# Two-direction SSD in a two-block network: one decay matrix from C.B masked twice, in place of a logarithm and mask matmuls

## The reference

```python
a_cs = jnp.cumsum(a_dt, axis=-1)
xdt = x * dt[..., None]
decay = segsum_exp(a_dt)          # exp(a_cs[l] - a_cs[s]) where s <= l, else 0
cb = jnp.einsum('bclgn,bcsgn->bcgls', c, b)
y_diag = jnp.einsum('bcgls,bcgrls,bcsgrp->bclgrp', cb, decay, xdt)
```

## Time and profile before

| | |
|---|---|
| median of 3 runs | 1795.68 us |
| the profiled execution | 1796.72 us |
| its span, first to last instruction | 1794.5 us |
| TensorE busy | 1771.6 us, 99% |
| VectorE busy | 834.1 us, 46% |
| ScalarE busy | 832.1 us, 46% |
| POOL busy | 811.4 us, 45% |
| mean granted clock of TensorE | 0.998 |

### The profile page before, as it was taken

The page is one execution under the profiler, slowest core; times in us unless marked ns, Lnnn a source line. Parts: engine busy times, 40 slices in busy tenths (PEclk is TensorE's granted clock), DMA queues, the critical chain, the costliest instruction groups (busy, mean ns, idle before and its releaser), DMA issues.

```text
span 1794.5 us, 26559 instructions
## 1 busy us (share of the span) xinstructions
PE 1771.6 (99%) x8872; PEld 1486.0 (83%) x8872; DVE 834.1 (46%) x1476; ACT 832.1 (46%) x1775; POOL 811.4 (45%) x598
## 2 busy tenths in 40 slices
PE   8999999999999999999999999999999999999998
PEld 7888888887888888888888888878888888888887
DVE  4687887878304554235440044050063312355763
ACT  4655555555425665325332233254534442367662
POOL 4553444466443222434654455445364444543322
PEclk9999999999999999999999999999999999999999
DMA  5732221221233221423333333324232223322211
GB/s 181 136 100 63 67 70 60 68 61 58 71 105 112 77 71 54 146 82 94 97 102 95 97 102 95 94 82 167 80 106 89 86 83 94 106 64 70 71 48 59
DMA packets 46227, 159.90 MB, mean 89 GB/s; under 512 B 4764, under 2 KB 7196, under 8 KB 45885
## 3 DMA queue, kind: packets, MB, share of 16 engines
q1 hardware_dynamic: 38592, 140.53, 25.3%
q10 hardware_dynamic: 7548, 18.20, 4.0%
HBM read 152.42 MB, written 6.29 MB: 88 GB/s over the span
## 4 chain that ended last, share of the span: by engine, by line
PE 86%; DVE 6%; issue 4%; ACT 2%; DMA 1%; POOL 0%; DVEq 0%; ACTq 0%; POOLq 0%
PE main L307 63%; PE main L335 6%; PE aux L810 3%; PE main L1875 2%; PE aux L797 2%; DVE u_acc L2081 1%; PE aux L657 1%; PE aux L379 1%; PE aux L781 1%; PE aux L780 1%; PE aux L665 1%; PE aux L1964 1%; PE aux L630 1%; PE aux L633 1%; DVE x_res L571 1%
## 5 line engine op out<-in xcount | busy, mean ns | idle before, releaser
L270 POOL TENSOR_TENSOR w_lo<-raw,w_hi 128x512 fp32r<-128x512 f32 x504 | 688.0, 1373 | 865.3 <-ACT w_hi L266 860.7
L266 ACT ACTIVATE w_hi<-raw 128x512 fp32r<-128x512 f32 x486 | 303.5, 630 | 653.1 <-PE main L307 646.7
L307 PE MATMUL main<-w_hi,a_hi 128*128 128x512 f32 x736 | 304.5, 414 | 1.4 <-ACT gu L1627 0.9
L307 PE MATMUL main<-w_hi,a_lo 128*128 128x512 f32 x736 | 287.8, 391 | 0.0
L307 PE MATMUL main<-w_lo,a_hi 128*128 128x512 f32 x736 | 287.1, 390 | 0.0
L307 PE MATMUL main<-a_hi,w_hi 128*128 128x512 f32 x576 | 230.7, 401 | 0.3 <-DVE relu L2280 0.3
L307 PE MATMUL main<-a_hi,w_lo 128*128 128x512 f32 x576 | 224.8, 390 | 0.0
L307 PE MATMUL main<-a_lo,w_hi 128*128 128x512 f32 x576 | 224.3, 389 | 0.0
L307 PEld LDWEIGHTS main<-w_hi,a_lo 128*128 128x128 f32 x736 | 138.1, 188 | 30.1
L307 PEld LDWEIGHTS main<-w_hi,a_hi 128*128 128x128 f32 x736 | 138.6, 188 | 27.2 <-issue 2.0
L307 PEld LDWEIGHTS main<-w_lo,a_hi 128*128 128x128 f32 x736 | 138.9, 189 | 22.9
(11 more groups left out here) (344 smaller groups left out, 3069.6 us busy)
## 6 DMA issues: line engine op xcount, KB each, us to landing
raw<-w_stream_in SPq DMA_DIRECT2D x264, 512.0 KB, 3.6
x_res<-x_in ACTq DMA_DIRECT2D x8, 512.0 KB, 5.3
rel_rows<-rel_row ACTq DMA_DIRECT2D x1, 4096.0 KB, 44.4
bias<-rel_rows ACTq DMA_DIRECT2D x2, 1536.0 KB, 7.8
out<-x_res SPq DMA_DIRECT2D x4, 512.0 KB, 2.6
bgate<-b_gate_in ACTq DMA_DIRECT2D x4, 256.0 KB, 5.4
ln_g<-ln_g_in ACTq DMA_DIRECT2D x1, 1024.0 KB, 6.2
ln_b<-ln_b_in ACTq DMA_DIRECT2D x1, 1024.0 KB, 9.6
```

The lines of the kernel that those rows point to most:

```text
L266: eng.activation(w_hi[:, k, :], raw[:, k, :], ACT.Copy).then_inc(hi_done, 1)
L270: eng.tensor_tensor(w_lo[:, k, :], raw[:, k, :], w_hi[:, k, :].bitcast(F32), ALU.subtract).then_inc(lo_done, 1)
L307: mm = eng.matmul(mb[m][:, :], lhs, rhs, start=(first and k == 0 and n == 0), stop=(last and k == KT - 1 and n == 2))
```

## The change

The decay matrix is built from the smaller of the two unmasked arguments. Forward and backward arguments have opposite signs off the diagonal, and on it both are 0; so the smaller one is the valid one of its side, and on the diagonal it is 0 and counts for both. The logarithm of dt, its clamp, the identity copy and the two mask tiles go, and so do the two L630 matmuls of each head. `cs_sb` is now the negated cumulative sum.

C.B is multiplied by the upper and by the lower mask, both with the diagonal, as it is read from bank 3: `mask_cb` has two operations of 128x512 where `take_cb` had a copy and seven small ones. ScalarE's new `scale_cb` multiplies the first by the forward dt, in four activations of 128x128 for each head, into a first half of `dmat[r]`, which is now two tiles. VectorE's `weigh` adds the second times the backward dt, in four operations of 128x128, waits for its own end, and then multiplies by the decay. POOL takes `d_skip` from the parameters and no longer waits for `skip_set`.

In ScalarE's order `scale_cb` of the next group's head 0 stands before the turned X tiles, of head 1 before argument 2, of head 2 after exponential 1; head 3's comes after argument 3 of the group itself. Buffers move within the space of the stage. The core of the diff:

```diff
-            for dr, neg in enumerate((neg_f, neg_b)):
-                eng.matmul(ab[dr][:, :].rearrange("p (c l) -> p c l", c=NT), ident_r[:, :],
-                           neg[:, :].unsqueeze(1).broadcast_to((P, NT, P)), start=True, stop=False)
+            for dr in range(2):
                 one_row = picked[:, half, dr, r:r + 1].broadcast_to((P, P))
-                x = eng.matmul(ab[dr][:, :], one_row, cs_hl[:, :], start=False, stop=True)
+                x = eng.matmul(ab[dr][:, :], one_row, cs_hl[:, :], start=True, stop=True)
...
-                pool.wait_ge(skip_set, g + 1)
+                skip = par[:, bass.ds(g * R + PC["d_skip"], R)].unsqueeze(1).unsqueeze(3).broadcast_to((P, NT, R, HP))
...
-            act.wait_ge(clamped, 1)
-            act.activation(ln_dt[:, :, :], sp_t[0][:, :, :], ACT.Ln).then_inc(ln_set, 1)
...
+            def scale_cb(g, r):
+
+                act.wait_ge(cb_set, g + 1)
+                if not (isinstance(g, int) and g == 0):
+                    act.wait_ge(y_full, g * 4 + (r - 3))
+                for c in range(NT):
+                    cs = slice(c * P, c * P + P)
+                    x = act.activation(dmat[r][:, 0, cs], cb_m[:, 0, cs], ACT.Copy, scale=dt_sb[:, c, bass.ds(g * R + r, 1)])
+                x.then_inc(cb_scaled, 1)
...
             decay_exp(0, 0)
             decay_exp(0, 1)
+            scale_cb(0, 0)
+            scale_cb(0, 1)
+            scale_cb(0, 2)
...
                 decay_exp(g, 2)
                 take_arg(g, 3)
+                scale_cb(g, 3)
...
                     slots(11, 12)
+                    scale_cb(g + 1, 0)
                     take_turned(g + 1, 2)
                     take_turned(g + 1, 3)
+                    scale_cb(g + 1, 1)
                     take_arg(g + 1, 2)
                     decay_exp(g + 1, 1)
+                    scale_cb(g + 1, 2)
...
-            dve.tensor_scalar(t[0], dt_sb[:, :, :], 1e-37, None, ALU.max).then_inc(clamped, 1)
-            dve.tensor_scalar(ident_r[:, :], ident, 1.0, None, ALU.mult).then_inc(neg_set, 1)
-            dve.tensor_scalar(neg_f[:, :], mask_u, -NEG, NEG, ALU.mult, ALU.add).then_inc(neg_set, 1)
-            dve.tensor_scalar(neg_b[:, :], mask_u, NEG, None, ALU.mult).then_inc(neg_set, 1)
...
-            def take_cb(g):
+            def mask_cb(g):
 
                 dve.wait_ge(turned, g * 4 + 2)
-                dve.tensor_copy(cb[:, :], ab[3][:, :]).then_inc(aux_free[1], 1)
...
+                for dr, mask in enumerate((mask_u, mask_l)):
+                    i = dve.tensor_tensor(cb_m[:, dr, :].rearrange("p (c l) -> p c l", c=NT), ab[3][:, :].rearrange("p (c l) -> p c l", c=NT),
+                                          mask.unsqueeze(1).broadcast_to((P, NT, P)), ALU.mult)
+                    i.then_inc(aux_free[1] if dr else cb_set, 1)
...
                 def weigh(r):
+                    dve.wait_ge(cb_scaled, g * 4 + r + 1)
+                    for c in range(NT):
+                        cs = slice(c * P, c * P + P)
+                        x = dve.scalar_tensor_tensor(dmat[r][:, 0, cs], cb_m[:, 1, cs], dt_sb[:, c, bass.ds(g * R + (NH + r), 1)],
+                                                     dmat[r][:, 0, cs], ALU.mult, ALU.add)
+                    ch(x)
                     dve.wait_ge(decay_done, g * 4 + r + 1)
-                    dve.tensor_tensor(dmat[r][:, :], cb[:, :], dmat[r][:, :], ALU.mult).then_inc(t_done, 1)
+                    dve.tensor_tensor(dmat[r][:, 0, :], dmat[r][:, 0, :], dmat[r][:, 1, :], ALU.mult).then_inc(t_done, 1)
```

More of the change, by code:

```diff
@@ L154, in two_blocks @@
         c_st = at("c_st", B0 + 6 * KB, [P, TOK])
[L155 to L159, removed]
+        cb_m = at("cb_m", B0 + 8 * KB, [P, 2, TOK])
         sz = at("sz", B0 + 12 * KB, [P, NT, NCOL])
-        dmat = [at(f"dmat{h}", B0 + (22 + 4 * h) * KB, [P, TOK]) for h in range(R)]
+        dmat = [at(f"dmat{h}", B0 + (20 + 4 * h) * KB, [P, 2, TOK]) for h in range(R)]
         xw = at("xw", B0 + 44 * KB, [P, 2, NT, GW])
@@ L665, in pe_y @@
                 x = eng.matmul(ab[c // 2][:, (c % 2) * GW + r * HP:(c % 2) * GW + r * HP + HP],
-                               dmat[r][:, c * P:c * P + P], x_tok[:, c, r * HP:r * HP + HP], start=True, stop=True)
+                               dmat[r][:, 0, c * P:c * P + P], x_tok[:, c, r * HP:r * HP + HP], start=True, stop=True)
             x.then_inc(y_full, 1)
@@ L2085, in conv, with arg_min @@
                             ch.count(ins)
-            def take_cb(g):
+            def mask_cb(g):
                 dve.wait_ge(turned, g * 4 + 2)
-                dve.tensor_copy(cb[:, :], ab[3][:, :]).then_inc(aux_free[1], 1)
-                dve.wait_ge(aux_free[1], g * 5 + 1)
-                dve.tensor_copy(dt_b[:, :, :], dt_sb[:, :, bass.ds(g * R + NH, R)])
-                for c in range(NT):
-                    own = dve.tensor_tensor_reduce(cb_own[:, c, :], cb[:, c * P:c * P + P], ident, 1.0, 0.0, ALU.mult, ALU.add, cb_d[:, c:c + 1])
-                ch(own)
-                ch(dve.tensor_tensor(skip[:, :, :], cb_d[:, :].unsqueeze(2).broadcast_to((P, NT, R)), dt_b[:, :, :], ALU.mult))
-                dve.tensor_tensor(skip[:, :, :], skip[:, :, :], par[:, bass.ds(g * R + PC["d_skip"], R)].unsqueeze(1).broadcast_to((P, NT, R)),
-                                  ALU.add).then_inc(skip_set, 1)
-            def arg_max(g, r):
+                for dr, mask in enumerate((mask_u, mask_l)):
+                    i = dve.tensor_tensor(cb_m[:, dr, :].rearrange("p (c l) -> p c l", c=NT), ab[3][:, :].rearrange("p (c l) -> p c l", c=NT),
+                                          mask.unsqueeze(1).broadcast_to((P, NT, P)), ALU.mult)
+                    i.then_inc(aux_free[1] if dr else cb_set, 1)
+            def arg_min(g, r):
                 dve.wait_ge(arg_in, g * 4 + (r + 1))
                 for c in range(NT):
-                    e = dmat[r][:, c * P:c * P + P]
+                    e = dmat[r][:, 1, c * P:c * P + P]
                     x = dve.scalar_tensor_tensor(e, ab[1][:, c * P:c * P + P], cs_sb[:, c, bass.ds(g * R + (NH + r), 1)], e,
-                                                 ALU.add, ALU.max)
+                                                 ALU.add, ALU.min)
                 x.then_inc(arg_done, 1)
             conv(0, 0, 0)
-            arg_max(0, 0)
+            arg_min(0, 0)
             conv(0, 0, 1)
-            arg_max(0, 1)
-            take_cb(0)
+            arg_min(0, 1)
+            mask_cb(0)
             def group_ms(g0, g1):
@@ L2161, in take_off @@
                         ch(dve.tensor_tensor(y, y, off_t[:, n % 2, :], ALU.add))
-                arg_max(g, 2)
+                arg_min(g, 2)
                 weigh(0)
-                arg_max(g, 3)
+                arg_min(g, 3)
                 weigh(1)
@@ L2196, in ssd_group @@
                 if not last:
-                    arg_max(g + 1, 0)
+                    arg_min(g + 1, 0)
                 dve.wait_ge(bank_free, gp * 12 + (4 * O_Z + 4))
@@ L2201, in ssd_group @@
                 if not last:
-                    arg_max(g + 1, 1)
-                    take_cb(g + 1)
-            per = len(TILES) * 3 + 2 + 2 + 3 + 6 + 1
+                    arg_min(g + 1, 1)
+                    mask_cb(g + 1)
+            per = len(TILES) * 3 + 4 + 2 + 3 + 6 + 1
             with dve.Fori(0, 3) as gp:
```

16 lines of the change are left out of this document (5 added, 11 removed).

## The result

The changed kernel takes 1848.28 us (median of 4 runs, 1847.12 to 1850.10) against 1795.74 of the kernel before (4 runs): ratio 1.0295 [1.028, 1.031], 52.5 us slower. The forecast was 1836, range 1809 to 1858. The profiled execution took 1850.1 us with a span of 1848.3, at a mean granted clock of 0.982.

The account below looks back on a forecast made before the run. Bound: TensorE, 99% busy, beside an equally long loop through ScalarE and VectorE. Groups add 36.9 us, less 0.9 at the start, plus 4 of blocking: +40 on 1796.72 gives 1836.7, 1.0 over the median, so 1836; range 1809 to 1858.

Parts of the forecast that it names:

- a second loop of equal length: In the SSD stage: `pe_arg(1)`, 13.3 us of ScalarE, 29.8 us of VectorE, `pe_turn(1)`; work added there is paid in full.
- zero slack at its end: At `pe_turn(1)`, start 213.97: TensorE waits for VectorE's last off-diagonal read, ended 213.84, with nothing to spare.
- TensorE alone: Rival: only TensorE's work decides, so 64 mask matmuls less save 14.7 us, giving 1781; chance 0.05.
- ScalarE's term: Scaling of three heads queued before `take_arg(3)`, 1.15 us a head, makes it 3.45 us later.
- VectorE's term without blocking: Four added operations and a wait per weighing, 1.27 us a head; heads 1, 2 and 3 in the loop: 3.81 us.
- the blocking by POOL: VectorE's added operations with two SBUF inputs lose time beside POOL: 4 us in all, between none and 12.9.
- already paid: In even groups POOL's catch-up was said to be in the 3.31 us of two weighings, so blocking was taken nearer to none.
- The place of the stall: TensorE idle before L646, `pe_off(0)` and `pe_arg(3)`, released by VectorE, some 8 us in an even group.
- the clock rival: A 3.3 us stall at `pe_off(0)` in even groups halves TensorE's clock: +12 over four groups, 1848; chance 0.10.
- an L646 with no more idle time than now: Sign of being wrong: no added TensorE idle time before the C.B matmul.
- A clock below 1.0: Sign of being wrong: a granted clock below 1.0 in the SSD stage.
- The mask gain: Mask matmuls between `pe_turn(1)` and `pe_arg(1)` save 0.46 us a group, and 0.9 more in the first group: 4.6 us.

Follow-up runs that it names:

- adds_early: The changed kernel with VectorE's additions of heads 0 and 1 moved ahead of the third argument, same work: 1840.78 us, ratio 1.0252.
- gap_scale2: The changed kernel with head 0's addition before the third argument, head 1's before the fourth, and ScalarE's scaling of head 2 behind the fourth: 1840.97 us, ratio 1.0251.

## Why the prediction was right, and where it was off

**The sign and the mechanism held.** The reasons were a second loop of equal length through ScalarE and VectorE, and zero slack at its end. The masks alone gave nothing, the two halves of the added work added up (13.1 + 37.3 against 51.4), all of it lies in the SSD stage, and the odd groups' idle time before the convolution is gone (9.2 us in four waits in the kernel before, group 0's among them; no such wait after). An even and an odd group together are 12.3 us longer (groups 2 and 3: 7.4 + 4.9), forecast 10 to 11. TensorE alone (1781) was not right for the changed kernel even with most of the blocking away (1803.6); it came near only for the masks alone, and only then (1777.8).

**ScalarE's term was right, by two errors that cancel.** 3.45 us forecast, 3.49 measured in group 2, where ScalarE works without a pause. But the 1.15 per head was read as the length of a row of four; what a queue pays is start to start, 1.00 for `take_arg` (190.79 to 191.79). The scaling is 1.17 (187.50 to 188.67), dearer by 0.17 for four, 0.04 each. The Trainium skill, VectorE: DVE Perf Modes, section on the TRN2 errata, has 52 cycles more for a ScalarE read from SBUF than from PSUM, by an estimate from its figures 0.04 us; the trace agrees (0.04, or 397 against 362 ns).

**VectorE's term without blocking** was a little high: from an addition's start to the product's it is 1.16 or 1.17 us (203.76 to 204.92), not 1.27; for three heads and 8 groups some 2.4 us less.

**The step that was mis-sized is the blocking by POOL.** I took 4 us, between 0 and 12.9, "nearer to none". The two stretches of the loop, measured as above in every group, show where it went: ScalarE's from the start of `take_arg(1)` to the end of `take_arg(3)`, and VectorE's from the start of its last argument to the end of the last states. The numbers say by how much a stretch is longer than before, in us; the last column is the growth of the blocking within VectorE's.

| group | ScalarE, forecast | ScalarE, measured | VectorE, forecast | VectorE, measured | blocking, more by |
|---|---|---|---|---|---|
| 0 | 2.6 | 2.1 | 3.2 | 3.0 | 0.0 |
| 1, 3, 5 (each) | 2.5 | 2.2 | 1.0 | 4.5 | 3.9 |
| 2, 4 (each) | 3.5 | 3.5 | 3.8 | 4.6 | 1.1 |
| 6 | 3.5 | 3.5 | 3.8 | 7.9 | 5.5 |
| 7 | 2.2 | 2.0 | 3.8 | 6.1 | 3.0 |
| sum | 22.8 | 21.1 | 21.3 | 39.7 | 22.4 |

VectorE's stretches are 18.4 over the forecast, ScalarE's 1.6 under it, and the half clock ahead of the output panel adds 1.1: 17.9, as many as are missing. That it closes to a tenth is partly luck, for these stretches are not the whole loop. But the pattern of the first table is there: the odd groups and the last two are the ones that were priced too low.

The additions are a part of it: over 0.34 us each they lose 19.3, 11.5, 4.2 and 0 us for heads 0, 1, 2 and 3. Head 0's falls where VectorE waits anyway; heads 1 to 3 have 15.7 in the loop. The rest is in operations that were there before: in group 6 the first convolution runs 10.07 us instead of 5.36, since POOL's work now lies beside it, and in the odd groups the convolution loses 2.1 instead of 1.1 and a product of the states 1.1 instead of none.

The reason for taking 4 was that POOL's catch-up in even groups was "already paid" in the two weighings. There it held: in groups 2 and 4 the weighings of VectorE's stretch lost 2.3 us before, and they and the additions together lose 2.1 now. What failed is that I carried it over to the other groups. In groups 1, 3 and 5 the weighings lost next to nothing before, and the additions lose 2.2; in group 7 the weighings lost 2.8, and they and the additions lose 6.9. The Trainium skill, SBUF — State Buffer, section Who interferes with whom, was the better guide: by its rule I had 1845, and 1848 was measured; L2099 against L2122 and the run with POOL only writing agree with it. The 12.9 us behind that 1845 were a price from other operations, so that it came so near is partly luck too.

What is shown is that with little blocking the same added work costs 25.8 instead of 51.4 us.

**The place of the stall was wrong.** I put it at the C.B matmul (`pe_turn(1)`), some 8 us in an even group together with `pe_off(0)` and `pe_arg(3)`; only the clock rival had a figure for `pe_off(0)`, 3.3. It is at `pe_off(0)`: 4.16 us in group 2, with 1.06 at the fourth argument, 0.68 at the third turn and 0.60 at the third states, 6.5 together. `pe_turn(1)` starts at 232.33, 0.98 after VectorE's read was done at 231.35, and between the two TensorE works through its own stretch without a wait. I had named an L646 with no more idle time than now as a sign that I was wrong. It was a bad sign to choose: two stations of the same loop lie 13.5 us apart, and either can carry the wait.

**The clock fell, and cost nearly nothing.** The rival was right in its event (4.2 to 6.3 us of standstill in seven groups, then 1.2 GHz; with group 7 54.6 us of the stage in all) and its 12 us were wrong: with 37.5 of the 54.6 us back at full clock the time is the same. The other 17.1 us were not tested; 1.1 us in group 7 can be seen to be paid. A clock below 1.0 was the other sign that I had named as one against me, and it proved nothing either.

**The mask gain** (4.6 us) can't be found alone. Taken out alone, the masks leave VectorE's and POOL's work in other places against each other, and the blocking grows by 14 us.

What stays open: how it comes about which of VectorE's and POOL's operations fall together. Edits of the queues that do the same work moved the blocking between 63 us (`adds_early`) and 82 (`gap_scale2`), against 72 in the changed kernel, which is as much as most of the edits were worth. No version found here beats the kernel before with the whole computation in it.

## What to carry to other kernels

An engine that is busy 99% can hide a second loop of the same length through other engines: before work is moved off it, measure the time from one of its hand-overs round to the next, and look for a place where the wait is zero. Price an added operation by what it takes in the company that it will have (here 0.62 us where 0.34 is its free time), and count starts, not lengths, in a queue. Ask of each added operation whether its inputs are both in SBUF and what the other engine that reads SBUF is doing at that time.

## What was not expected of the hardware

- What VectorE loses beside POOL doesn't go away with the operations that lose it: 72 us with four short additions a head, 73 with one long one, 66 in the kernel before without any. Most of it went over to the next operation. It is no constant either: 55 without the additions, 84 without the scaling.
- POOL writing the same tiles without reading them blocks little: 72 to 29 us, and 44.7 us of the kernel's time. None of the 33 additions that overlap such a write is long.
- Removing 64 matmuls from an engine that is 99% busy gained 0 us (ratio 1.0007). Once POOL read less, the same kernel took 19.1 us less.
- 37.5 us at half clock, waits included, on the busiest engine cost nothing measurable (1847.92 without them against 1848.28).
